# Attention: probability copies ahead of exponentials and transposes one unit later, and the scaling of the second component on GpSimd

## The reference

```python
def one_block(args):            # 128 queries
    sc = jnp.einsum('bqhcd,bkhcd->bhcqk', q_blk, k).astype(jnp.float32) * scale
    allowed = key_chunk[None, :] <= q_chunk[:, None]       # chunks of 64 keys
    sc = jnp.where(allowed, sc, jnp.finfo(jnp.float32).min)
    p = jax.nn.softmax(sc, axis=-1)
    p_diff = p[:, :, 0] - lam * p[:, :, 1]
    return jnp.einsum('bhqk,bkhe->bqhe', p_diff.astype(v.dtype), v)
```

## Time and profile before

| | us |
|---|---|
| median of 3 runs (3218.14 to 3227.24) | 3220.45 |
| the profiled execution | 3212.86 |
| its span, first to last instruction | 3211.0 |
| TensorE busy in the span | 2963.3 |
| VectorE busy | 1552.7 |
| ScalarE busy | 1035.1 |
| GpSimd busy | 418.1 |
| attention: first score matmul | 886.2 |
| attention: last copy of `op` | 1370.2 |

### The profile page before, as it was taken

One profiled execution on the slowest core, in us unless ns is written; L12 is line 12 of the kernel. 1 busy time (PEld: TensorE's weight loads), 2 busy tenths in 40 slices (PEclk: granted clock), 3 DMA queues, 4 the chain that ended last, 5 costly groups with the idle time before them and its releaser, 6 DMA issues. The chain is left out here.

```text
span 3211.0 us, 66008 instructions
## 1 busy us (share of the span) xinstructions
PE 2963.3 (92%) x25434; PEld 1895.5 (59%) x25435; DVE 1552.7 (48%) x3592; ACT 1035.1 (32%) x2431; POOL 418.1 (13%) x620
## 2 busy tenths in 40 slices
PE   8999999999778888879999988999599999999999
PEld 6777777878545555578888874555233333333333
DVE  5676767777667677623333337786211111111111
ACT  3344334433367777722222222333100000000000
POOL 0000000000000000000000000000233333333333
PEclk9999999999989999989999999999699999999999
DMA  6121212111211000041111112334488888877663
GB/s 235 60 73 60 68 59 70 60 63 56 84 65 40 24 17 1 1 147 45 45 44 44 45 37 79 105 105 171 122 300 300 303 293 297 300 256 264 249 245 117
DMA packets 190196, 397.46 MB, mean 124 GB/s; under 512 B 16154, under 2 KB 76442, under 8 KB 188912
## 3 DMA queue, kind: packets, MB, share of 16 engines
q1 hardware_dynamic: 169440, 343.47, 30.4%
q0 software_dynamic: 20512, 50.54, 4.6%
HBM read 327.25 MB, written 80.32 MB: 127 GB/s over the span
## 5 line engine op out<-in xcount | busy, mean ns | idle before, releaser
L325 PE MATMUL pj_big<-pj_xnT,pj_w_in 128*128 128x256 f32 x2816 | 633.3, 381 | 4.3 <-ACT pj_ubuf L397 2.8
L325 PEld LDWEIGHTS pj_big<-pj_xnT,pj_w_in 128*128 128x128 f32 x2816 | 536.3, 191 | 85.1 <-ACT pj_ubuf L397 6.7
L1806 PE MATMUL ex_pgu<-keep_res,ex_xT 128*64 128x512 f32 x2560 | 569.3, 597 | 0.0
L1806 PEld LDWEIGHTS ex_pgu<-keep_res,ex_xT 128*64 128x64 f32 x2560 | 177.3, 137 | 335.2 <-issue 335.2
L1914 DVE TENSOR_TENSOR ex_hh<-ex_sg,ex_pgu 128x256 f32<-128x256 f32 x80 | 33.7, 421 | 584.3 <-ACT ex_sg L1879 584.3
L1824 PE MATMUL ex_py<-keep_res,ex_hT 128*64 128x512 f32 x1280 | 288.3, 592 | 1.0 <-DVE ex_yb L1922 1.0
L1325 PE MATMUL mg_po<-keep_res,mg_mix 128*128 128x512 f32 x512 | 232.4, 611 | 6.9 <-DVE mg_mix L1628 6.9
L737 ACT ACTIVATE at_e<-at_sc,at_nmx 128x512 f32<-128x512 f32 (+3 forms) x320 | 196.4, 620 | 111.7 <-DVE at_nmx L776 111.5
L776 DVE TENSOR_REDUCE at_nmx<-at_sc 128x2 f32<-128x1024 f32 (+3 forms) x160 | 170.2, 1063 | 102.8 <-PE at_sc L699 67.9
L1879 ACT ACTIVATE ex_sg<-ex_pgu 128x256 f32<-128x256 f32 x80 | 30.7, 383 | 581.6 <-PE ex_pgu L1806 581.6
L723 PE MATMUL at_op<-at_vh,at_pt 128*128 128x128 f32 x1088 | 161.5, 289 | 49.6 <-ACT at_pt L755 49.0
(11 more groups left out here) (293 smaller groups left out, 4761.1 us busy)
## 6 DMA issues: line engine op xcount, KB each, us to landing
keep_res<-in_w_exp_gate SPq DMA_DIRECT2D x32, 2048.0 KB
keep_res<-in_w_exp_up SPq DMA_DIRECT2D x32, 2048.0 KB
keep_res<-in_w_exp_down SPq DMA_DIRECT2D x32, 2048.0 KB, 8.8
chunks_s<-pj_st SPq DMA_DIRECT2D x32, 642.0 KB, 3.7
rw_raw<-chunks_s SPq DMA_DIRECT2D x32, 642.0 KB, 3.9
pj_xt<-in_x SPq DMA_DIRECT2D x20, 512.0 KB, 3.6
qk_s<-pj_qo SPq DMA_DIRECT2D x64, 128.0 KB, 1.9
mg_xin<-in_x SPq DMA_DIRECT2D x8, 1024.0 KB, 6.8
```

The costliest lines, as they stand in the source:

```text
L325: ins = pe.matmul(out, lhs, rhs, start=(k == 0), stop=(k == KC - 1))
L1806: ins = pe.matmul(pgu[j * BT:(j + 1) * BT, :, :], lhs, wgu[x][:, k, :, j * HE:(j + 1) * HE], start=(k == 0), stop=(k == KC - 1))
```

## The change

The order of the steps is written anew. The turn of a unit comes one step later (unit k-8 in step k) and stands ahead of soft in the list, so ScalarE's copy to `pt` is issued ahead of the exponentials of unit k. Values and out come one step later as well (unit k-9), and the list has one more step at its end. And "scale" is no longer an instruction of ScalarE but a `tensor_scalar` of GpSimd with the same operands and waits. Buffers and all other waits are unchanged.

```diff
-    for k in range(NU + LAG + 2):
+    for k in range(NU + LAG + 3):
         if k < NU:
             steps += [("scores", k)]
         tile_ends = 1 <= k <= NU and (k == NU or UNITS[k][1] == 0)
         if tile_ends:
             steps += [("maxima", UNITS[k - 1][0])]
+        if 0 <= k - LAG - 2 < NU:
+            steps += [("turn", k - LAG - 2)]
         if k < NU:
             steps += [("soft", k)]
...
-        if 0 <= k - LAG - 1 < NU:
-            steps += [("turn", k - LAG - 1)]
-        if 0 <= k - LAG - 2 < NU:
-            u = k - LAG - 2
+        if 0 <= k - LAG - 3 < NU:
+            u = k - LAG - 3
...
-                if kind == "scale":
-                    (t, s), w = UNITS[u], width(u)
-                    act.wait_ge(s_cf, t + 1)
-                    after(act, s_pd, u - 1)
-                    act.activation(tt[:, u % 2, 0:w], e[:, u % RE, 1, 0:w], ACT.Copy,
-                                   scale=cf[:, t % RE, 1, s:s + 1]).then_inc(s_t, 1)
...
+        @block.gpsimd
+        def _(pool):
+            for kind, u in STEPS:
+                if kind == "scale":
+                    (t, s), w = UNITS[u], width(u)
+                    pool.wait_ge(s_cf, t + 1)
+                    after(pool, s_pd, u - 1)
+                    pool.tensor_scalar(tt[:, u % 2, 0:w], e[:, u % RE, 1, 0:w], cf[:, t % RE, 1, s:s + 1], None,
+                                       ALU.mult).then_inc(s_t, 1)
```

## The result

The changed kernel takes 3129.44 us (median of 4 runs, 3125.98 to 3131.39) against 3220.52 of the kernel before (median of 4, 3218.14 to 3227.24). The ratio is 0.9715 with a 95% interval of 0.970 to 0.973: 91 us faster. The forecast was 3154, in a range of 3132 to 3190.

A forecast was written before the change was run, and what follows sets the result against it. A loop of waits between TensorE and ScalarE, 3.06 us a unit, was taken as the bound. Heads 1 to 3 give 56, the first 12, less 1.4 for the end: 66 us, so 3154, range 3132 to 3190.

The forecast's parts named there:

- the loop: Attention: TensorE waits for ScalarE's copy to pt, ScalarE for the maxima; 6.12 us for two units, 3.06 each.
- GpSimd's latency: Scaling on GpSimd: its result is needed two units on, some 4.4 us later, so it lies on no path.
- the floors: Tile groups of a head with both engines, TensorE and VectorE, unwaiting: 12.2, 18.0, 27.8, 38.0 us, 96 a head.
- the first head: Attention's first head fills the pipeline and began on a lower clock; its gain was taken as 12 us.
- the hold: VectorE's two-input operations wait until GpSimd ends: six tile differences a head, some 0.45 us each, about 1.4 on the path.
- changes of pace: Shifts of pace between engines in a head's groups: 0.6 us for two-unit, 1.2 for three-unit, 1.0 added for four-unit tiles.
- one-unit tiles: First four tiles of a head: VectorE already the bound, floor 12.2 us as measured, forecast 12.7 after the change.
- Rival (b): Each step from tile to tile costs 0.5 us more, 8 a head, through queueing behind VectorE; 3183 us; chance 0.10.
- X: GpSimd's time for one full scaling of 512 columns: taken as 0.7 us, kept between 0.6 and 2.1.
- Rival (a): GpSimd's scaling takes a two-input operation's 1.45 us, holding VectorE longer; saving 50 us, giving 3170; chance 0.20.
- signs of being wrong: Scalings above 1.8, longer combines, VectorE waiting for tt, TensorE for exponentials at the scores, a long-tile group above 43 us.
- Rival (c): With X 2.1, combine and scaling exclude each other: some 8 us a head slower, 3252; from X about 1.8; chance 0.10.

The follow-up runs named there:

- At 2.2: Changed kernel plus a second GpSimd scaling of 128 columns for each unit into an unread spare buffer: 3130.76 us, a head 96.6.
- At 3.1: Changed kernel with GpSimd doing each scaling twice, the first into an unread spare buffer: 3201.26 us, a head 112.2.
- the first half alone: Changed kernel with the copy to pt still ahead of the exponentials, but transposes and values not a step later: 3155.01 us.
- the second half alone: Changed kernel with transposes and values still a step later, but the copy to pt behind the exponentials again: 3179.42 us.

## Why the prediction missed

**Right.** The mechanism was right: the loop, and the copy behind the exponentials as the place where it hung. The wait of 49.0 us fell to 0.8, and with the copy behind the exponentials again 50 us come back. GpSimd's latency lies on no path: VectorE waits for it 2.4 us in all. The extra step costs no more than the drain: head 3 and the end gained 22.7 us where each head before them gained 23.2. VectorE is late next in the short tiles, as moving its copy shows.

**Wrong: the sizes of the terms added on the floors.** These are the step of the prediction that failed: the first head's gain at 12 us, which measured 21.6, and the 4.2 us a head on top of the floors (1.4 for the hold, 2.8 for changes of pace), of which nothing is left in the measured 95.7 us against floors of 96.0. The gain in the attention is 90.8 instead of 66.4, 24.4 more, and splits thus:

| | gain forecast | measured |
|---|---|---|
| first head | 12 | 21.6 |
| heads 1 and 2 | 37.2 | 46.5 |
| head 3 and the end | 17.2 | 22.7 |

The first head was taken at 12 because it fills the pipeline on a low clock. No row carried that. Before and after, it lasts from the first score row (886.2 and 889.9) to the first maxima of head 1:

```profile
1001.25 0.42 DVE L776 TENSOR_REDUCE at_nmx<-at_sc 128x2 f32<-128x256 f32 x1
```

```profile
983.27 0.42 DVE L780 TENSOR_REDUCE at_nmx<-at_sc 128x2 f32<-128x256 f32 x1
```

Its one-unit tiles take 8.1 us in both kernels, and from there on it ran much like any other: 22.0, 36.9 and 46.9 before, 18.6, 28.2 and 37.3 after. The granted clock was low only at the start, 0.77 and 0.75 of full speed in the first windows of the two kernels, then 0.96 and 0.98:

```profile
886.00:920.00 34.00, 26.08 (x129) 16.09 (x131) 24.84 (x80) 21.99 (x71) 0.00 (x0) 0.77 0.37 119
...
889.90:910.00 20.10, 13.69 (x69) 8.32 (x69) 14.72 (x53) 10.88 (x42) 4.32 (x4) 0.75 0.55 179
```

That term alone was 9.6 us short. The other three heads were short by 4.6 us each, and the end took 0.5 instead of 1.4.

The lower end of the range, 3132, stood for both engines at their floors and a first head of 21: a gain of 88. The measured gain is 2.8 more: 0.6 in the first head, 0.9 in heads 1 and 2, and 1.3 in head 3 with the end.

In each head 2.8 us had been added for "changes of pace" (0.6, 1.2 and 1.0 for the groups). On top of the prediction's floors they don't show: the groups took 18.7, 28.2 and 37.3 against floors of 18.0, 27.8 and 38.0, 0.4 more in sum. Rival (b), 8 us a head built on the same worry, falls with it.

That the floors of a head meet the measured time within 0.3 us is in part luck. The prediction counted a group's transposes and values with the group itself, but they run eight and nine units behind the scores. TensorE was busy in the four groups for 10.7, 17.6, 26.5 and 37.1 us, where it had 7.5, 17.6, 27.8 and 38.0; only the sums, 91.9 and 90.9, are near. (What was expected of the mixed tiles used the same 7.5.) In the three-unit tiles TensorE did stand idle for 1.7 us of 28.2, so changes of pace cost something there, and a floor 1.3 too high made up for it.

The hold was taken at 1.4 a head on the path for X = 0.7. For X = 1.45 the same reasoning gave 1.2 at six tiles and 0.3 at ten. In head 2 six differences are held, by 0.1 to 0.4 us each, 1.9 in sum, and two combines by 0.5 in sum; writing only instead of reading saves 1.0 a head. That the forecast's 1.4 is near this is luck too: X was taken too short, and the hold too long for its X.

And the one-unit tiles were set at the measured 12.2, since "there VectorE is already the bound". The prediction's own pieces give less: four times 1.43, 2.5 times 1.15 for the maxima and four combines of 0.67 are 11.3, and 11.5 was measured. VectorE was not the bound at the first of them: the timeline of before has a wait of 1.24 there, for the exponential of the tile's differences, which on ScalarE stood behind a scaling and a copy.

```profile
1240.69 0.17 DVE L788 TENSOR_TENSOR at_cf<-at_f,at_sums 128x8 f32<-128x8 f32 x1 [1.24 <-ACT at_f L744]
```

After the change this wait is 0.35 at the same place, which the forecast had not counted as a gain.

**Wrong with little effect: X.** It is 1.57 instead of 0.7. The nearest rows were a copy and one tiny operation, and "one input" was taken as the reason for a copy's rate. Rival (a) had nearly this X and would have missed by 41 us: it let the hold last as long as the operation, and used the small first head and the changes of pace as well. (Its groups sum to 104.3, not 104.5, which moves its time by less than 1 us.)

One of the signs of being wrong did appear, TensorE waiting for exponentials at the scores: 3.7 us in a head, and no loss against the forecast.

**Rival (c)** put the turning point at 1.8 through exclusion for the whole length. At 2.2 a head is 0.9 us longer. At 3.1 the time is that of GpSimd's own length (112.2 a head, expected 113 to 116) and far from 150.

## What to carry to other kernels

Where the engines of a pipeline wait for each other in turn, write out one round of the loop from start to start. Look for the step that is old work behind new work in an engine's queue. Here putting the old work first needed one more step of delay upstream: with the scaling on GpSimd, the first half alone left 26 us of the gain behind and the second half alone 50.

When floors of two engines have been worked out from rows and every dependence has slack, an allowance that no row carries should be marked as a guess, and the first turn of a loop is looked up in the trace like any other. A floor for a group of tiles counts the work that the engine does in that stretch, old units included. Where two engines take turns at being the bound by the size of the work, mix the sizes.

## What the runs showed of the hardware

- A GpSimd `tensor_scalar` in float32 with one input and a factor for each partition takes 0.60 us for 128 columns and 1.57 for 512, 2.5 ns a column; a filling of 512 columns 0.53; a copy of 1284 columns 1.25. So two operations with one input tile each differ in rate, and the number of inputs alone doesn't set it. The Trainium skill, GPSIMD Engine Reference, section 3.1, has 1.03 cycles an element for short bodies and about 2.6 for two inputs; from the first the prediction estimated X near 0.6. The measurement decides, and is 1.57.
- A two-input operation of VectorE with both inputs in SBUF that begins just behind a GpSimd scaling is held, but only for about the first third: until 0.54 us of a 1.56 us scaling of 512 columns, 0.37 of 1.24 for 384, 0.22 of 0.60 for 128. A filling doesn't hold it at all. The other way round, a scaling that began 0.03 us after a combine took 2.07 us instead of 1.56. The Trainium skill, SBUF — State Buffer, section "Who interferes with whom", names exactly these pairs and frees the GpSimd operation that only writes; the runs agree. It has the second instruction blocked until the first finishes; here the measurement decides, and says 0.54 of 1.56 us.
